# A join of two blocks in a one-core float32 network: squares summed by two-column products, chunks kept in two PSUM banks, one variance computed a gate earlier, a table load a unit earlier

## The reference

```python
# first block: RWKV branch and sparse attention branch, joined by an output product
y = jnp.concatenate([y_rwkv, y_attn], axis=-1) @ w_out
x = x + y
x = rmsnorm(x, final_g)                 # (x * rsqrt(mean(x^2) + 1e-6)) * final_g
# second block
h = _rmsnorm(x, norm_mix_g)             # a second norm of the normed x
proj = h @ w_in                         # p_a (gb, gc, v), p_b (u, ug), q, p_g
y_a = (gb * conv3(gc * v)) @ w_a_out
u = conv31(u * sigmoid(ug)) + conv_b_bias
u = silu(_layernorm(u, ln_b_g, ln_b_b)) # mean and variance over the 1024 channels
y_b = u @ w_b_out
k, vm = split(_rmsnorm(mem) @ w_kv, 2)  # 256 memory tokens, 4 heads
y_c = softmax(q k^T / 16) vm @ w_att_out
merged = g0 * y_a + g1 * y_b + g2 * y_c # g = sigmoid(p_g + b_gate)
x = x + merged @ w_o
x = x + (silu(gt) * up) @ w_down        # gt, up = conv3(rmsnorm(x) @ w_up)
out = _rmsnorm(x, norm_final_g)
```

## Time and profile before

| | |
|---|---|
| median of three runs | 1490.29 us |
| profiled execution | 1488.9 us |
| its span, first to last instruction | 1487.2 us |
| mean granted TensorE clock | 0.979 of full speed |
| PE busy | 1432.9 us, 96% |
| DVE, ACT, POOL busy | 65%, 34%, 33% |
| HBM read | 121.84 MB, 83 GB/s over the span |

### The profile page before, as it was taken

One profiled execution on the slowest core, in us unless ns is written; L12 is line 12 of the kernel. 1 busy time (PEld: TensorE's weight loads), 2 busy tenths in 40 slices (PEclk: granted clock), 3 DMA queues, 4 the chain that ended last, 5 costly groups with the idle time before them and its releaser, 6 DMA issues.

```text
span 1487.2 us, 18566 instructions
## 1 busy us (share of the span) xinstructions
PE 1432.9 (96%) x7552; PEld 1153.1 (78%) x7552; DVE 960.1 (65%) x1333; ACT 512.1 (34%) x710; POOL 488.6 (33%) x132
## 2 busy tenths in 40 slices
PE   7999988899998999999999999989989999999997
PEld 6778655687888887888888887768878888888886
DVE  6679788544646357669969973663357888884121
ACT  5443388553334323122222222322233333332221
POOL 0004121012534322343444433334333343443441
PEclk9999999999989999999999999999989999999998
DMA  6222000203333211223222232212221223222221
GB/s 203 85 85 85 1 2 1 87 2 114 116 112 113 83 59 57 85 87 112 85 102 97 88 111 69 91 68 93 106 85 62 108 85 114 85 100 92 95 82 57
DMA packets 21348, 125.12 MB, mean 84 GB/s; under 512 B 2384, under 2 KB 3408, under 8 KB 7696
## 3 DMA queue, kind: packets, MB, share of 16 engines
q1 hardware_dynamic: 20752, 121.71, 23.1%
q10 hardware_dynamic: 512, 2.23, 0.4%
HBM read 121.84 MB, written 2.10 MB: 83 GB/s over the span
## 4 chain that ended last, share of the span: by engine, by line
PE 84%; DVE 10%; ACT 3%; issue 1%; DMA 0%; POOLq 0%; POOL 0%; DVEq 0%; SPq 0%; ACTq 0%
PE bank L392 23%; PE bank L393 23%; PE bank L394 23%; DVE score L1874 2%; DVE misc L1873 2%; PE bank L627 1%; PE bank L967 1%; PE bank L983 1%; PE bank L344 1%; PE bank L374 1%; ACT w_hi L1215 1%; DVE op_lo L1721 1%; PE bank L585 1%; ACT prob L1369 1%; DVE conv_b L2362 1%
## 5 line engine op out<-in xcount | busy, mean ns | idle before, releaser
L1162 POOL TENSOR_TENSOR w_lo<-w_raw,w_hi 128x2048 fp32r<-128x2048 f32 (+1 forms) x102 | 467.1, 4579 | 814.8 <-ACT w_hi L1215 700.1
L392 PE MATMUL bank<-op_hi,w_hi 128*128 128x512 f32 x1344 | 531.0, 395 | 13.6 <-DVE op_lo L1700 6.7
L393 PE MATMUL bank<-op_lo,w_hi 128*128 128x512 f32 x1344 | 526.9, 392 | 0.0
L394 PE MATMUL bank<-op_hi,w_lo 128*128 128x512 f32 x1344 | 526.7, 392 | 0.0
L392 PEld LDWEIGHTS bank<-op_hi,w_hi 128*128 128x128 f32 x1344 | 254.1, 189 | 71.9 <-issue 11.3
L1215 ACT ACTIVATE w_hi<-w_raw 128x2048 fp32r<-128x2048 f32 (+2 forms) x109 | 205.7, 1887 | 282.1 <-PE bank L394 282.1
L394 PEld LDWEIGHTS bank<-op_hi,w_lo 128*128 128x128 f32 x1344 | 253.9, 189 | 54.6
L393 PEld LDWEIGHTS bank<-op_lo,w_hi 128*128 128x128 f32 x1344 | 254.1, 189 | 54.2 <-issue 0.7
L2254 DVE SCALAR_TENSOR_TENSOR bank<-pad_b,par,bank 128x512 f32<-128x512 f32 x232 | 175.3, 756 | 7.8
L2421 DVE TENSOR_TENSOR tmp<-tmp,conv_f 128x512 f32<-128x512 f32 x22 | 101.5, 4615 | 16.4 <-ACT tmp L1646 16.4
L2162 DVE TENSOR_TENSOR x_res<-bank,x_res 128x512 f32<-128x512 f32 x24 | 16.5, 691 | 108.8 <-PE bank L394 108.7
(11 more groups left out here) (368 smaller groups left out, 1761.6 us busy)
## 6 DMA issues: line engine op xcount, KB each, us to landing
w_raw<-in_w_units SPq DMA_DIRECT2D x104, 1024.0 KB, 4.8
w_raw<-in_w_units SPq DMA_DIRECT2D x4, 768.0 KB, 4.2
x_res<-in_x SPq DMA_DIRECT2D x8, 256.0 KB, 6.5
x_res<-in_x ACTq DMA_DIRECT2D x2, 1024.0 KB, 6.1
out<-x_res SPq DMA_DIRECT2D x8, 256.0 KB, 2.3
w_raw<-in_w_units SPq DMA_DIRECT2D x3, 512.0 KB, 9.1
w_raw<-in_w_units SPq DMA_DIRECT2D x4, 256.0 KB, 5.7
mem_tok<-in_mem SPq DMA_DIRECT2D x1, 1024.0 KB, 6.1
```

The costliest lines, as they stand in the source:

```text
L392: nc.tensor.matmul(b[:, 0:width], h, xh[:, x0 + k, 0:width], start=start and k == ks[0], stop=False)
L393: nc.tensor.matmul(b[:, 0:width], h, xl(x0 + k, width), start=False, stop=False)
L394: mm = nc.tensor.matmul(b[:, 0:width], l, xh[:, x0 + k, 0:width], start=False, stop=stop and k == ks[-1])
L1162: nc.gpsimd.tensor_tensor(w_lo[u % 2][:, 0:nk, :], w_raw[u % 2][:, 0:nk, :], w_hi[u % 2][:, 0:nk, :].bitcast(F32), ALU.subtract).then_inc( ...
```

## The change: what it does

It has six parts.

1. Sums of squares. sq_g goes, and so do the DVE additions at the join. ACT squares each chunk once. PE multiplies each of the eight chunks by a two-column operand sum_cols (ones, and final_g squared), which gives both sums at once, in bank 7 (`input_sums`). The products of chunks 0 to 3 stand behind wout units 1 and 2, those of chunks 4 to 7 behind wout unit 3.
2. The order on ACT behind wout unit 3: squares of chunks 6 and 7, then the root, then the split of weights, which stood first.
3. The spread of the joint root stands behind the first tile of kT unit 0 (`mix_spread`), and not behind its second.
4. The scaled chunks go to PSUM banks 6 and 5 (MIX_BANKS) in turn, and not to tmp; ACT and DVE read them there (`mixed_hi`, `mixed_lo`). ACT does two chunks behind each kT unit. The ring of banks is 0 to 4 meanwhile.
5. In branch 0 the variance is summed behind pg unit 2, before y unit 2. Chunks 0 and 1 then go between the tiles of y unit 2, chunks 2 to 5 behind it, 6 and 7 before y unit 3.
6. A Sqrt of one element stands on ACT behind the third unit of wout, wo2 and down, ahead of the root. At the end one chunk goes by ACT and POOL and seven by DVE; the stores are in the order 1, 2, 3, 4, 5, 0, 6, 7.

```diff
+            def input_sums(c):
+
+                if c == 0:
+                    pe.wait_ge(sem("sum_cols_ready"), 2)
+                pe.wait_ge(sem("sq_y"), c + 1)
+                for t in range(NT):
+                    mm = nc.tensor.matmul(ps[CONV_BANK][:, 2 * t:2 * t + 2], sq2[:, c, t * P:t * P + P], sum_cols[:, c, :],
+                                          start=c == 0 and t == 0, stop=c == CH - 1, skip_group_check=True)
+                if c == CH - 1:
+                    done(mm, "y")
+
...
-            token_sums("y", sq2)
-            token_sums("yg", sq_g)
+                if i:
+                    input_sums(2 * i - 2)
+                    input_sums(2 * i - 1)
+            input_sums(CH - 2)
+            input_sums(CH - 1)
+            for s, b in enumerate(MIX_BANKS):
+                ring.remove(b)
+                seq[("mix", s)] = b, used[b]
+
+            def mix_spread():
+                pe.wait_ge(sem("tok_both_ready"), 1)
+                seq["rs_mix"] = CONV_BANK, used[CONV_BANK]
+                used[CONV_BANK] += 1
+                pe.wait_ge(free[CONV_BANK], used[CONV_BANK] - 1)
+                spread("rs_mix", tok_mix, ps[CONV_BANK])
+
...
+                unit_tiles("kT", i, memn_hi, plain(memn_lo), MEM, between=None if i else mix_spread)
             unit_tiles("u", 0, oh, ol, ready="mixn_ready")
+            ring.extend(MIX_BANKS)
...
-                    unit_tiles("y", i, mh, ml, branch=branch, ready=None if i else operand)
-                    if branch == 2 and i:
-                        unit_tiles("u", 2 + i, oh, ol)
-                    if branch == 0 and i == 1:
-
-                        sum_chunks("ln_mean", conv_b, CH, T, "conv_ready")
                     if branch == 0 and i == 2:
                         b = bank("ln_var")
                         for c in range(0, CH, 2):
                             pe.wait_ge(sem("paired_ln"), c // 2 + 1)
                             mm = nc.tensor.matmul(b[:, :], ones[:, :], sq2[:, c, :], start=c == 0, stop=c == CH - 2)
                         done(mm, "ln_var")
+                    unit_tiles("y", i, mh, ml, branch=branch, ready=None if i else operand)
+                    if branch == 2 and i:
+                        unit_tiles("u", 2 + i, oh, ol)
+                    if branch == 0 and i == 1:
+
+                        sum_chunks("ln_mean", conv_b, CH, T, "conv_ready")
...
-            for c in (2, 3, 4, 0, 5, 6, 1, 7):
-                if c < 2:
-                    sp.wait_ge(sem("fin_pool"), c + 1)
+            for c in (1, 2, 3, 4, 5, 0, 6, 7):
+                if c == 0:
+                    sp.wait_ge(sem("fin_pool"), 1)
                 else:
-                    sp.wait_ge(sem("fin_ready"), c - 1)
+                    sp.wait_ge(sem("fin_ready"), c)
...
-            for c in range(2):
-                pool.wait_ge(sem("fin_gained"), c + 1)
-                nc.gpsimd.tensor_tensor(x_res[:, c, :], x_res[:, c, :], rs[:, :], ALU.mult).then_inc(sem("fin_pool"), 1)
+            pool.wait_ge(sem("fin_gained"), 1)
+            nc.gpsimd.tensor_tensor(x_res[:, 0, :], x_res[:, 0, :], rs[:, :], ALU.mult).then_inc(sem("fin_pool"), 1)
...
-                filled(act, ("wout", i, 1))
-                after_unit()
+                if i < 3:
+                    filled(act, ("wout", i, 1))
+                    after_unit()
+                if i == 2:
+                    A(misc[:, 127:128], ones[:, 0:1], ACT.Sqrt)
                 for c in (2 * i, 2 * i + 1):
                     evacuated(act, ("wout", i, c % 2))
                     A(sq2[:, c, :], x_res[:, c, :], ACT.Square).then_inc(sem("sq_y"), 1)
-                    A(sq_g[:, c, :], x_res[:, c, :], ACT.Square, scale=pcol("final_g", c)).then_inc(sem("sq_yg"), 1)
+            filled(act, ("wout", 3, 1))
             root(misc[:, 99:107], "tok_mix_ready")
+            after_unit()
+
+            def mixed_hi(c):
+                act.wait_ge(sem("mixn_scaled"), c + 1)
+                A(op_hi[:, c, :], ps[MIX_BANKS[c % 2]][:, :], ACT.Copy).then_inc(sem("mixn_hi"), 1)
 
...
-                if i:
-                    hi_chunks(((0, 1), (1, 3), (3, 5))[i - 1], "mixn")
-            hi_chunks((5, CH), "mixn")
+                mixed_hi(2 * i)
+                mixed_hi(2 * i + 1)
...
+                    if branch == 0 and i == 2:
+                        root()
+                        ln_sigmoids(0, 2)
                     if branch == 0 and i == 3:
-                        ln_sigmoids(2, 5)
+                        ln_sigmoids(6, CH)
                     filled(act, ("y", branch, i, 1))
...
+                    if branch == 0 and i == 2:
+                        ln_sigmoids(2, 6)
...
+                if i == 2:
+                    A(misc[:, 127:128], ones[:, 0:1], ACT.Sqrt)
...
-                if i:
-                    sum_squares("y", sq2, i - 1)
-                    sum_squares("yg", sq_g, i - 1)
-                else:
+                if i == 0:
+                    c0 = PARAM_AT["final_g"]
+                    V.memset(sum_cols[:, :, 0], 1.0).then_inc(sem("sum_cols_ready"), 1)
+                    V.tensor_tensor(sum_cols[:, :, 1], par[:, c0:c0 + CH], par[:, c0:c0 + CH], ALU.mult).then_inc(sem("sum_cols_ready"), 1)
                     dve.wait_ge(sem("x_res_loaded"), 32)
...
-            link(token_variance("y", 1.0 / D, NORM_EPS))
-            b = take(dve, "yg")
-            evac(V.tensor_tensor(tok_mix, b[:, 0:NT], tok_rs, ALU.mult), "yg")
-            evacuated(dve, "yg")
+            b = take(dve, "y")[:, 0:2 * NT].rearrange("p (t n) -> p n t", n=2)
+            link(V.tensor_scalar(tok_rs, b[:, 0, :], 1.0 / D, NORM_EPS, ALU.mult, ALU.add))
+            link(V.reciprocal(tok_rs, tok_rs))
+            evac(V.tensor_tensor(tok_mix, b[:, 1, :], tok_rs, ALU.mult), "y")
+            evacuated(dve, "y")
...
+            def mixed_lo(c):
+
+                dve.wait_ge(sem("mixn_hi"), c + 1)
+                V.tensor_tensor(op_lo[:, c, :], ps[MIX_BANKS[c % 2]][:, :], op_hi[:, c, :].bitcast(F32), ALU.subtract)\
+                    .then_inc(sem("mixn_ready"), 1)
...
             def mix_norm(c):
 
-                ins = V.scalar_tensor_tensor(tmp[c % 2][:, 0:T], x_res[:, c, :], both_g[:, c:c + 1], r_mix[:, :], ALU.mult, ALU.mult)
-                ins.then_inc(sem("mixn_scaled"), 1)
+                if c < 2:
+                    b, n = seq[("mix", c)]
+                    dve.wait_ge(free[b], n)
+                V.scalar_tensor_tensor(ps[MIX_BANKS[c % 2]][:, :], x_res[:, c, :], both_g[:, c:c + 1], r_mix[:, :], ALU.mult, ALU.mult)\
+                    .then_inc(sem("mixn_scaled"), 1)
                 if c:
-                    lo_chunk(c - 1, "mixn")
+                    mixed_lo(c - 1)
...
+                        variance("ln_var", T, 1.0 / D, EPS2)
                     if branch == 0 and i == 3:
...
-                        ln_silu(2, 5)
+                        ln_silu(6, CH)
                     for m in range(2):
+                        if branch == 0 and i == 2:
+                            ln_silu(m, m + 1)
...
                     if branch == 0 and i == 2:
-
-                        variance("ln_var", T, 1.0 / D, EPS2)
-                        ln_silu(0, 2)
-                    if branch == 0 and i == 3:
-                        ln_silu(5, CH)
+                        ln_silu(2, 6)
...
-            for c in range(2, CH):
+            for c in range(1, CH):
```

27 lines of the change are left out of this document (11 added, 16 removed).

## The result

The changed kernel takes 1476.17 us (median of 4 runs, 1475.13 to 1477.98), the kernel before beside it 1492.91 (1489.78 to 1497.62): ratio 0.9887, 95% interval 0.9853 to 0.992. The forecast was 1477.2 from 1490.29, a ratio of 0.991, with a range of 1471.8 to 1482.6; the intervals reach 0.2 to 0.3% to either side, so neither tells the forecast from a gain 2 to 3 us larger or smaller. The profiled execution took 1475.13 us with a span of 1473.4, where before had 1488.9 and 1487.2.

What follows compares the result with a forecast made beforehand. TensorE, 96% busy, was taken to bound the kernel, so gains must come from its waits or half-clock time. Join 6.5 + layer norm 5.6 + end 1.0 = 13.1 us off 1490.29 gave 1477.2, range 1471.8 to 1482.6.

Steps and rivals of the forecast that it cites:

- The join: From wout to unit u 0: new order and two-column sums start u 0 sooner; 6.5 us gained, 4.9 to 7.8.
- one short fall of the clock: Behind the sixteen product pairs before kT unit 0: half clock costs first kT tiles 1.5 us, u 0 starts 1.3 later.
- two waits of 1.3: At the join, PE was to wait about 1.3 us for weights ahead of kT units 1 and 3.
- The layer norm: Branch 0's earlier variance sum lets y unit 0 of branch 1 end sooner; about 5.6 us gained, 4.0 to 9.0.
- a second chain of holds: Layer norm: chunk 2's first step also caught by POOL, 943.0 not 941.4; y unit 0 ends 981.2, not 980.2.
- half a fall of the clock: Branch 1's y unit 0: a fall behind the 2.3 us wait would cost 1.6; half of it was taken.
- The end: Last normalization and stores: seven chunks on DVE, transfers packed without a hole; 1.0 us gained, 0.5 to 1.3.
- The table loads: Early Sqrt loads on ACT: the load was already covered, so moving it gains nothing; 0 us.
- No hold and no fall at all: Rival across join, layer norm and end: no POOL holds, no clock fall; 18.1 us gained, 1472.2; chance 0.14.
- Layer norm nothing: Rival: pg unit 0 of branch 1 waits for late weights, layer norm gives 0; 7.5 us gained, 1482.8; chance 0.14.
- Join 3: Rival: weights bind the join sooner, it gives 3 us; sum 9.6, 1480.7; chance 0.11.
- Slower by a clock that stays at 1.2 GHz: Rival: two-column products behind wout units 1 and 2 keep later units slow, 9.5 us each; 1496.2; chance 0.05.

## Why the prediction was right

- **The join, 6.5 forecast, 6.2 measured** (6.1 by timing the part alone, and 5.5 to 7.7 by the pairs of profiles, so the 0.3 says little). The terms came as written: 0.91 a chunk, one short fall of the clock behind the last pairs (the bound without it was 7.8), u 0 without a wait for a chunk, low parts of 0.69, rs_y 0.69. The weights are the exception: two waits of 1.3 were forecast and four were there, 2.1 in all, of which 1.4 had been there before. Choosing the row with PE busy at half clock over the rule of the Trainium skill, "TensorE: Matmul & The Clock Gate", section "Part 1: The HAM clock gate", was right: by that rule, if busy is what the profile calls so, this join gives 7.8, and the trace, at 0.50 with PE busy 2.00 of 2.00, disagrees. What the monitor itself counts no run here shows.
- **The layer norm, 5.6 forecast, 7.05 measured.** This term was mis-sized, inside its bounds of 4.0 and 9.0, and its parts were off by more than their sum. Too low: the sum has a slip (987.3 - 981.5 is 5.8 and not 5.6), 981.5 holds 0.5 for a second chain of holds and 0.8 for half a fall of the clock, of which neither came, and the wait was 1.66 and not 2.3, on the sixth chunk and not the fifth. That makes 0.2 + 0.5 + 0.8 + 0.64 = 2.1. Too high by 0.7: the unit's 48 matmuls were put at 48 x 0.23 to the start of ACT's split, which came 0.69 later than that, as the matmuls stood 0.232 apart and the last one has to end. The difference is the 1.45. Held steps were four, as reckoned.
- **The end, 1.0 forecast, 0.76 in the profile of the part alone**, too small to time. Of the 2.1 in the changed kernel's own profile 1.3 is the clock, at a place where the forecast had none.
- **The table loads, 0 forecast, between 0.6 less and 3.3 more by the interval.** The sum by the drain of 1.38 us in the Trainium skill ("ScalarE: Activation LUTs", "What ACT_TABLE_LOAD costs"), 0.5 less, can't be told from 0 by timing. The trace disagrees with the drain: the root starts 0.21 behind DVE with and without a load, and ACT's next operation 0.02 behind the end of a load.
- **The rivals.** No hold and no fall at all: holds of 4.2 to 4.8 and a fall are in the trace. Layer norm nothing: weights of pg unit 0 were split at 944.17, and PE did not wait. Join 3: stage A is 5.5 to 7.7 shorter. Slower by a clock that stays at 1.2 GHz: it came back within 6 us in the changed kernel (1.00 from 446 on), and by 450 even with all 64 products from 436.24 on.

The terms were off by -0.3, +1.45 and -0.24 for the parts. The sum of 13.1 stands against 16.8 and 13.3 by the ratios of two timings and 13.8 in the first profile, where 1.3 of the clock at the end and 1.5 lost ahead of the join, neither of them forecast, cancel nearly. The mechanism held in the main; the closeness of the total is in part luck.
